# Latent normalisations moved inside the opening projections, and context rows fetched a stage ahead, in a two-model transformer kernel

## The reference, cut to what matters

```python
def hybrid_layer(x, ctx, ...):
    h_lat = rms_norm(x, norm_g) * (1.0 + scale) + shift
    h_ctx = rms_norm(ctx, norm_g) * (1.0 + scale_c) + shift_c
    qc, kvc, kr, dq, dk, dv, sq, sk, sv, z, gm = split_cols(h @ w_in)   # both of h_lat, h_ctx
    # branch 1 (mla), from the low-rank latents qc (384) and kvc (256)
    q = rms_norm(qc, q_norm) @ w_uq          # 8 heads x (64 + 32)
    kv = rms_norm(kvc, kv_norm) @ w_ukv      # 8 heads x (64 + 128)
    ya = dense_attend(...)
    # branch 2 (diff): 8 heads, two softmax maps each
    # branch 3 (swa): 16 query heads, 4 key/value heads of 64, window 128 plus the context
    x = x + gate * (sum_r sigmoid(gm_r) * ((y_r * silu(z_r)) @ w_branch[r])) @ w_out
    # the same for ctx in layer 0
```

## Time and profile before

| | before |
|---|---|
| median of 3 runs | 4311.13 us (4303.09 to 4312.06) |
| profiled execution | 4305.82 us, span 4304.0 us |
| granted TensorE clock, mean over the span | 0.951 |
| PE busy | 3832.1 us (89%) |
| DVE busy | 2169.0 us (50%) |
| ACT busy | 1391.3 us (32%) |
| DMA, mean | 64 GB/s |

### The profile page before, as it was taken

How to read it: one execution, slowest core, us unless ns; L and a number is a source line. 1 busy time by engine, 2 the same in 40 slices (tenths; PEclk the granted TensorE clock), 3 DMA queues, 4 the chain that set the end, 5 groups by cost and what they waited for, 6 DMA issues and landing times. The chain is left out here.

```text
span 4304.0 us, 56060 instructions
## 1 busy us (share of the span) xinstructions
PE 3832.1 (89%) x20877; PEld 2926.4 (68%) x20877; DVE 2169.0 (50%) x3457; ACT 1391.3 (32%) x2476; POOL 0.2 (0%) x4
## 2 busy tenths in 40 slices
PE   4988979998689999999798998977999999798998
PEld 2655758876457787777586666865667777576666
DVE  3555345543455525777524555243563677535544
ACT  2433233322233313444312443121332444314432
POOL 0000000000000000000000000000000000000000
PEclk8999999998899999999899999988999999899999
DMA  6443325531100121111121101211103111121122
GB/s 234 139 113 94 92 83 166 163 115 69 35 25 24 33 61 45 39 34 34 35 64 33 27 25 31 68 39 38 33 28 84 52 45 39 54 69 30 35 59 73
DMA packets 504242, 275.36 MB, mean 64 GB/s; under 512 B 56665, under 2 KB 489781, under 8 KB 504094
## 3 DMA queue, kind: packets, MB, share of 16 engines
q1 hardware_dynamic: 483186, 252.08, 20.7%
q10 hardware_dynamic: 20908, 21.26, 1.6%
HBM read 271.08 MB, written 10.32 MB: 65 GB/s over the span
## 5 line engine op out<-in xcount | busy, mean ns | idle before, releaser
L559 PE MATMUL ps<-h_high,w_high 128*128 128x512 f32 (+1 forms) x3512 | 1309.5, 373 | 173.7 <-DVEq L2341 129.8
L559 PE MATMUL ps<-h_low,w_high 128*128 128x512 f32 (+1 forms) x3512 | 1279.0, 364 | 0.0
L559 PE MATMUL ps<-h_high,w_low 128*128 128x512 f32 (+1 forms) x3512 | 1275.5, 363 | 0.0
L559 PEld LDWEIGHTS ps<-h_high,w_high 128*128 128x128 f32 x3512 | 672.1, 191 | 324.6 <-DVEq L2341 137.2
L555 DVE TENSOR_TENSOR w_low<-w_raw,w_high 128x1024 fp32r<-128x1024 f32 x378 | 453.8, 1201 | 642.5 <-ACT w_high L545 618.7
L559 PEld LDWEIGHTS ps<-h_high,w_low 128*128 128x128 f32 x3512 | 671.2, 191 | 105.8
L559 PEld LDWEIGHTS ps<-h_low,w_high 128*128 128x128 f32 x3512 | 672.3, 191 | 96.6 <-issue 2.2
L545 ACT ACTIVATE w_high<-w_raw 128x1024 fp32r<-128x1024 f32 x378 | 392.2, 1039 | 784.8 <-PE ps L559 606.6
L781 ACT ACTIVATE probs<-ps,neg_max 128x768 f32<-128x768 f32 (+2 forms) x368 | 289.5, 789 | 641.5 <-DVE neg_max L806 441.2
L559 PE MATMUL ps<-probsT,v 128*128 128x512 f32 (+4 forms) x736 | 286.9, 559 | 10.3 <-DVE probsT L999 8.8
L559 PE MATMUL ps<-k_high,q_high 64*128 64x256 f32 (+4 forms) x784 | 185.9, 397 | 116.1 <-ACT probs L781 57.9
(11 more groups left out here) (200 smaller groups left out, 4030.4 us busy)
## 6 DMA issues: line engine op xcount, KB each, us to landing
w_raw<-in_w_in SPq DMA_DIRECT2D x444, 256.0 KB, 3.1
y_and_merged<-in_w_mod SPq DMA_DIRECT2D x96, 256.0 KB, 3.1
w_raw<-in_w_branch SPq DMA_DIRECT2D x96, 256.0 KB, 3.0
w_raw<-in_w_up SPq DMA_DIRECT2D x88, 256.0 KB, 4.2
y_and_merged<-in_w_ada SPq DMA_DIRECT2D x64, 256.0 KB, 3.3
w_raw<-in_w_out SPq DMA_DIRECT2D x48, 256.0 KB, 3.0
w_raw<-in_w_down SPq DMA_DIRECT2D x44, 256.0 KB, 2.8
y_and_merged<-in_w_ada SPq DMA_DIRECT2D x4, 2048.0 KB, 21.0
```

The lines of the kernel that those rows point to most:

```text
L559: return nc.tensor.matmul(*a, **kw)
```

## The change

It has five parts.

1. The stages `qn` and `kvn` go. Their work is done inside `pre`: ScalarE squares a latent row (`act_square`) once it is copied out, TensorE sums the query rows behind block 3 and the key rows behind the rotation (`pe_latent`), ScalarE takes the roots (`act_latent`), VectorE the reciprocals and the scaling (`dve_latent`), for the queries behind the copy of block 4 and for the keys at the stage's end. The rows are scaled at 512 or 768 columns in one instruction. The first mla unit waits for the query latents ahead of its q, for the key latents ahead of its k.
2. The stages `ctxload` go. ScalarE issues the loads at the start of `down` (for layer 0's norm) and of the last `merge` of layer 0 (for `out`); the transposes and copies come in `gfinal` and in `out` of layer 0.
3. `swapre` has four blocks for six: two for the keys, 128 columns each, and ScalarE and VectorE each copy their 64 partitions of the result twice.
4. `fence` counts each engine on a semaphore of its own, and TensorE doesn't wait at the end of `h1`, `h2`, `layer` and `pre`. Its first block behind a norm waits for each row of `h_low` (semaphore `low_row`) in its place.
5. In `h2` and `layer`, VectorE makes the `w_low` of the first block ahead of its wait for the root.

```diff
-    st += [Stage("norm", what="gfinal", nk=8, size=D, ctx=False)]
+    st += [Stage("norm", what="gfinal", nk=8, size=D, ctx=False, rows=True)]
...
-        if cq:
-            st += [Stage("ctxload")]
         st += [Stage("norm", what="layer", nk=8, size=D, ctx=True, l=l)]
         st += [Stage("pre", **com)]
-        st += [Stage("norm", what="qn", nk=3, size=384, ctx=cq, l=l), Stage("norm", what="kvn", nk=2, size=256, ctx=True, l=l)]
...
-                for g in range(4):
-                    src = win2[l][:, :, C_SK + 64 * g:C_SK + 64 * g + 64]
-                    load_split(sp, s, 0, 0, g, [((slice(0, 8), slice(64 * a, 64 * a + 64)), src) for a in range(2)])
-                for j in range(2):
-                    load_split(sp, s, 0, 0, 4 + j, cols(win2[l], C_SV + 128 * j))
+                for j, c in enumerate((C_SK, C_SK + 128, C_SV, C_SV + 128)):
+                    load_split(sp, s, 0, 0, j, cols(win2[l], c))
...
-                        pe.wait_ge(S[ready], s.base[ready] + k0 + kc + 1)
+                        pe.wait_ge(S[ready], s.base[ready] - since + k0 + kc + 1)
...
             if name == "mla":
+                if not ahead:
+                    pe.wait_ge(S["lat_n"], s.base["lat_n"] - 1)
...
+                else:
+                    pe.wait_ge(S["lat_n"], s.base["lat_n"])
                 for lo, n, ps in tgroups(2, True, 64):
...
+        def pe_rows(pe, s):
+            pe.wait_ge(S["ctx_in"], s.base["ctx_in"] + 32)
+            for j in range(4):
+                for e in range(2):
+                    for a in range(2):
+                        kc = 2 * j + e
+                        last = nc.tensor.transpose(bank(4 + j, 128, 256 * e + 128 * a), SQ_ROWS[:, a, 128 * kc:128 * kc + 128], ident[:, :])
+                last.then_inc(S["x_t"], 1)
...
+        def act_rows(act):
+            c = w["ctx_2"][0].rearrange("(a p) d -> p a d", p=128)
+            for a in range(2):
+                act.dma_start(SQ_ROWS[:, a, :], c[:, a, :]).then_inc(S["ctx_in"], 16)
...
+            if s["what"] in ("h2", "layer"):
+                dve_low(dve, Stage("first", h_end=None).at(s.base), 0, 0, 0)
             dve.wait_ge(S["rstd"], s.base["rstd"] + 1)
...
+                last.then_inc(S["low_row"], 1)
                 v.drain()
...
+        def pe_latent(pe, s, g):
+            for kc in LROWS[g]:
+                pe.wait_ge(S["lat_sq"], s.base["lat_sq"] + kc + 1)
+                for lo, n, ps in latent_parts(s, g, kc):
+                    last = mm(ps, ones[:, :], LSQ[:, kc, lo:lo + n], start=kc == LROWS[g][0], stop=kc == LROWS[g][-1], skip_group_check=True)
+            last.then_inc(S["lat_ss"], 1)
+        def act_square(act, s, j):
+            act.wait_ge(S["mm_ev"], s.base["mm_ev"] + 8 + j + 1)
+            n = TOK if j >= 3 or s["cq"] else LAT
+            act.activation(LSQ[:, j, 0:n], M[:, j, 0:n], ACT.Square).then_inc(S["lat_sq"], 1)
+        def act_latent(act, s, g):
+            act.wait_ge(S["lat_ss"], s.base["lat_ss"] + g + 1)
+            for lo, n, ps in latent_parts(s, g, 0):
+                last = act.activation(LRS[:, g, lo:lo + n], ps, ACT.Sqrt, scale=1.0 / (128 * len(LROWS[g])), bias=EPSB[:, :])
+            last.then_inc(S["lat_rs"], 1)
+        def dve_latent(dve, s, g):
+            n = TOK if g == 1 or s["cq"] else LAT
+            dve.wait_ge(S["lat_rs"], s.base["lat_rs"] + g + 1)
+            v.reciprocal(LRS[:, g, 0:n], LRS[:, g, 0:n])
+            v.drain()
+            for kc in LROWS[g]:
+                last = v.scalar_tensor_tensor(out=M[:, kc, 0:n], in0=M[:, kc, 0:n], scalar=VT[:, at:at + 1], in1=LRS[:, g, 0:n], ...)
+            last.then_inc(S["lat_n"], 1)
...
             elif k == "out":
+                if s["ctx"]:
+                    pe_rows(pe, s)
...
-                    pe_split(pe, s, 0, 0, j, m, tgroups(2 * (j % 2), s["cq"] or j >= 3, m))
+                    pe_split(pe, s, 0, 0, j, m, tgroups(2 * (j % 2), s["cq"] or j >= 3, m), ready="low_row" if j == 0 else None, since=8)
+                    if j == 3:
+                        pe_latent(pe, s, 0)
...
+                pe_latent(pe, s, 1)
...
             elif k == "down":
+                act_rows(act)
...
             elif k == "pre":
                 for j in range(6):
                     act_high(act, s, 0, 0, j + 1)
+                    if j:
+                        act_square(act, s, j - 1)
+                    if j == 4:
+                        act_latent(act, s, 0)
+                act_latent(act, s, 1)
             elif k == "swapre":
-                for j in range(6):
+                for j in range(4):
                     act_high(act, s, 0, 0, j + 1)
+                    if j < 2:
+                        act.wait_ge(s_h, s.base["h"] + j + 1)
+                        b = 1024 * (j % 2)
+                        for e in range(2):
+                            last = act.activation(KB[64 * e:64 * e + 64, 2 * j, :], PS[0:64, b:b + TOK], ACT.Copy)
+                        last.then_inc(S["k_out"], 1)
...
                     v.tensor_tensor(HL[:, kc, 0:nn], M[:, kc, 0:nn], HR[:, kc, 0:nn].bitcast(F32), ALU.subtract).then_inc(S["m_low"], 1)
+                if s["ctx"]:
+                    dve_rows(dve, s)
+                    v.drain()
...
                     last.then_inc(S["mm_ev"], 1)
+                    if j == 4:
+                        dve_latent(dve, s, 0)
...
+                dve_latent(dve, s, 1)
...
-                    if j < 4:
-                        v.tensor_copy(KB[:, j, :], PS[:, 512 * b:512 * b + TOK]).then_inc(S["mm_ev"], 1)
+                    if j < 2:
+                        for e in range(2):
+                            last = v.tensor_copy(KB[64 * e:64 * e + 64, 2 * j + 1, :], PS[64:128, b:b + TOK])
+                        last.then_inc(S["mm_ev"], 1)
...
-        def fence(eng, s):
-            eng.drain().then_inc(s_fence, 1)
-            eng.wait_ge(s_fence, 3 * (s.index + 1))
+        def fence(eng, me, s):
+            eng.drain().then_inc(s_fence[me], 1)
+            if me == "pe" and (s.kind == "pre" or s.kind == "norm" and s["what"] in ("h1", "h2", "layer")):
+                return
+            for other in s_fence:
+                if other != me:
+                    eng.wait_ge(s_fence[other], s.index + 1)
```

100 lines of the change are left out of this document (51 added, 49 removed).

## The result

| | before | changed kernel |
|---|---|---|
| median | 4309.58 us (4303.09 to 4312.06, 4 runs) | 4201.02 us (4200.46 to 4203.57, 4 runs) |
| ratio, 95% interval | | 0.9752 (0.9735 to 0.9768) |
| profiled execution, span | 4304.0 us | 4198.7 us |
| granted TensorE clock | 0.951 | 0.959 |
| PE busy | 3832.1 us (89%) | 3807.2 us (91%) |

The time is the predicted one, 4202, to within 1 us. The experiments are about that.

A forecast was written before the change was run, and what follows sets the result against it. It took serial chains between stages, where TensorE stands idle, as the bound. Its terms, 33.3 + 22.9 + 20.9 + 6 + 5 + 5 + 0 + 6.5 - 0.9 + 7.5, gave 106.2 us saved: 4202 us, 8 in 10 for 4184 to 4222.

The forecast's parts named there:

- The scale: Whole kernel: 4199.6 us on the profiled execution's scale, 4204.9 on the median's; 4202 was said.
- swapre, 33.3: swapre, both layers: four projection blocks of 8.33 us go, 33.3 us saved, the added copies hidden under a block.
- Latents, layer 0, 22.9: Layer 0, block 4's copy to first k_high: 56.3 us becomes 29.5, less 3.9 for sums; 22.9 saved, 20.0 to 25.8.
- ready by then: Layer 0, end of pre: ScalarE's root of the second norm at 16.0 us, before VectorE needs it at 16.4.
- Latents, layer 1, 20.9: Layer 1, block 5's copy to k_high: 41.5 us becomes 18, less 2.6 for sums; 20.9 saved, 17.9 to 23.0.
- Heads, 6 + 5 + 5 + 0: First projections behind norms, TensorE taking h_low row by row: 6 us layer 0, 5 layer 1, 5 h2, 0 h1.
- the sign that I named: In the profile after, first blocks of the heads end 3.5 to 7 us behind the last h_low.
- h1: Norm h1 into dil: 4.5 us won at 78 us, lost to an unmoved raw-weight transfer; 0, at best 4.5.
- the 9.5 I named: TensorE's wait by dil's second unit: near 9.5 us rather than 5.04 in the profile after.
- Context rows, 6.5 and 7.5: Removed ctxload stages: first load saves 6.5 us after 2.5 for transposes; second, with out, 7.5, between 5.5 and 9.2.
- The DMA issue in down: Start of down: ScalarE issues two context transfers ahead of the first f_high TensorE awaits, costing 0.9 us.
- The rule on waits: Waits between matmul pieces make TensorE run cold: heads and key parts take their low ends, sum 95 us.

The follow-up runs named there:

- after_again: The changed kernel, unedited, timed and profiled a second time: 4201.5 us, ratio 0.9744 to the kernel before.
- ctx_stages: The changed kernel with both ctxload stages put back: 4216.3 us, ratio 0.9783 to the kernel before.
- best: The changed kernel with SP issuing dil's bias-table copy in eight pieces, pre's key rotation behind the key latents, and down's context-row loads issued later: 4183.75 us.
- pe_waits: The changed kernel, but TensorE again waits at the ends of h1, h2 and both layer norms: 4213.6 us, ratio 0.9776 to before.
- the filled wait: The changed kernel with key sums ahead of the rotation, first-unit w_low later, and five unread products in TensorE's wait for the key latents: 4199.1 us.

## Why the prediction held, step by step

- **The scale.** The working gave 4199.6 on the profiled execution's scale and 4204.9 on the median's, and I stood between. The saving was 106.2 by my sum, 108.6 by the medians above and 110.5 in after_again's group. The profiled execution of before had the early start and the changed kernel's the late one: the spans differ by 105.3 us, and with the starts alike it would be 110.8. So the sum was 2 to 5 us short; on the median's scale alone I would have said 4204.9, and 3 us of the hit are owed to the step toward the other scale. That the profiled execution stood 5.3 us under the median had a reason, and by the three early profiles it was the start.
- **The misses cancel.** Against the prediction's terms five stretches of the table gave 9.0 us more (h2 to down 1.2, gfinal 2.9, the norm of layer 0 0.5, its latents 2.0, out 2.4) and four 10.2 less (the start 5.5, swapre of layer 0 1.4, swa 1.3, layer 1 2.0). That the time came within 1 us is luck; that it came within the range is not.
- **swapre, 33.3:** right (33.4 alone in the kernel before). The cover for the copies was as said.
- **Latents, layer 0, 22.9:** 24.9 by marks, 23.8 undone. The chain on VectorE came out to 0.6 us (24.6 for 24), with two misses in it: the root was not "ready by then" but 1.64 us late behind sums at the low clock, and the scaling, in one instruction for each row, took 2.88 and 1.95 us for 3.26 and 2.2. The key part ran high, not between (2.79 us), and k_high came at 27.5 us for the 29.5 I took.
- **Latents, layer 1, 20.9:** 41.5 less 18.4, less 2.6 for the sums (block 4 ended 10.9 us behind block 3, for 8.3), is 20.6; 19.3 undone. The key part ran low.
- **Heads, 6 + 5 + 5 + 0:** 6.5 in layer 0, 6.3 for h2 and up (the stretch's 5.3, with what down lost, 1.0, put back), and 3.3 in layer 1 (23.9 less the 20.6 above), where block 1 paid 2.8 us of low clock (8.2 for 5.4); I had allowed up to 2.0. As a sum, right, since h2 made up for layer 1. Of the sign that I named, first blocks that end 3.5 to 7 us behind the last h_low, layer 0 shows it (1099.43 to 1105.28); in layer 1, without context columns, it was 1.8 us.
- **h1: the result right, the step wrong.** I wrote that the transfer "is issued when the second w_low of dil is done, which the change does not move". It does: that w_low went from 87.97 to 82.1 us, and the load's issue from 89.22 to 83.35. The landing moved by 1.1 us only (w_high at 103.25 for 104.36), since the issue took 9.72 us for 3.49. Nor were 4.5 us won at 78 us: dil's second block took 7.4 us for 5.4 at the low clock, and k_high came 2.4 us sooner (89.42 for 91.83). So TensorE's wait became 6.30 us, 5.04 and 2.4 less 1.1, not the 9.5 I named, and 1.1 us came through. The large copy was there to be seen in the trace of before, issued at 78.77 us, and I didn't ask what else the rings held.
- **Context rows, 6.5 and 7.5:** mis-sized, 9.4 and 9.9 (9.0 and 10.1 undone). I charged 2.5 us for transposes that cost 0.7 at most, and 1.7 in out, where TensorE then stood at a higher clock (1.00 for 0.89). Behind gfinal the clock was lower than without the change (0.76 over 1060 to 1073, for 0.87 over 1062 to 1075 in ctx_stages), and the norm of layer 0 with its block 0 lasts 1.6 us longer than there. The DMA issue in down was 0.9 as said, and down as a whole 1.0 to 2.2; in best, where it is issued later, h2 to down takes 1.9 less.
- **The rule on waits.** By the Trainium skill, "TensorE: Matmul & The Clock Gate", section "Loop structure matters more than you think", a "long DMA wait between every matmul" makes TensorE go cold. I applied it to waits of any length, which the section does not say; the waits here are short. In the layer norms TensorE does stay at the low clock: with waits of 0.65 us and one trio for each 2.30 us, a trio's first matmul lasts 0.80 us. In h2 it does not: with one trio for each 1.50 us it lasts 0.79 us at first and 0.50 from the fifth on. And in pre a wait of 3.81 us was followed by 2.79 us of work in the changed kernel and by 4.49 for the same work in ctx_stages and pe_waits. The sum that I drew from the rule, 95 us, was too low; and the low ends that I listed with it add to 97.5, not 95.

```profile
1098.20 0.80 PE L553 MATMUL ps<-h_high,w_high 128*128 128x512 f32 x1 [0.65 <-DVE h_low L1838]
```

```profile
628.80 0.50 PE L553 MATMUL ps<-h_high,w_high 128*128 128x512 f32 x1 [0.54 <-DVE h_low L1838]
```

The first is layer 0 in the changed kernel, the second h2 in after_again. Open is what sets the place of the low stretch in pre: the filled wait shows that it isn't that wait alone.

## What to carry to other kernels

When a stage end goes, sum what stood in its chain and place it anew in the queue of the engine that was the chain: that sum came out to 3 us a piece or better, and the next gain was found in the same queue (put what TensorE waits for ahead of what only ScalarE waits for). A wait for a transfer asks two questions, when it was issued and what was in the rings then; here the length of the issue itself in the trace (9.72 us for about 1) gave the second away. And price each term against a second execution where one is to be had: here an early or a late start moved a profile by 5 us, as much as a whole term.
